# Low halves behind the residual, gains of the second attention folded into other steps, and a new order of head work, in a two-block transformer kernel

## What is computed

```python
def diff_mixer(h, cos, sin, w_in, w_out, q_norm, k_norm, lam_params, out_norm, lam_init):
    q, k, v = jnp.split(h @ w_in, [qk_w, 2 * qk_w], axis=-1)
    q = partial_rope(rms_norm(q.reshape(...), q_norm), cos5, sin5)   # 8 heads x 2 maps of 64
    k = partial_rope(rms_norm(k.reshape(...), k_norm), cos5, sin5)   # first 16 of 64 columns turned
    lam = exp(sum(lp[0] * lp[1])) - exp(sum(lp[2] * lp[3])) + lam_init
    p = masked_softmax(q k^T * scale, causal)
    a = p[:, :, 0] - lam * p[:, :, 1]
    o = rms_norm(a @ v, out_norm) * (1.0 - lam_init)
    return o @ w_out
```

## Time and profile before

| | us |
|---|---|
| median of 3 runs | 1537.43 |
| profiled execution, its own time | 1539.54 |
| its span | 1537.7 |
| PE busy | 1461.9 (95%) |
| DVE busy | 1060.2 (69%) |
| ACT busy | 757.7 (49%) |

### The profile page before, as it was taken

The page is one execution under the profiler, slowest core; times in us unless marked ns, Lnnn a source line. Parts: engine busy times, 40 slices in busy tenths (PEclk is TensorE's granted clock), DMA queues, the critical chain, the costliest instruction groups (busy, mean ns, idle before and its releaser), DMA issues.

```text
span 1537.7 us, 21173 instructions
## 1 busy us (share of the span) xinstructions
PE 1461.9 (95%) x8545; PEld 1185.5 (77%) x8545; DVE 1060.2 (69%) x1637; ACT 757.7 (49%) x1208; POOL 0.2 (0%) x4
## 2 busy tenths in 40 slices
PE   5998999999998899999989999989999998999997
PEld 3777778888786567787768888778888886788886
DVE  4586768886769866566576655688877897476555
ACT  3454554344544554334446554465546635465543
POOL 0000000000000000000000000000000000000000
PEclk9999999999999999999999999999999999999999
DMA  9875367876465758875855755568876523246551
GB/s 363 302 257 219 111 200 253 284 275 232 152 246 194 245 193 294 300 274 201 299 193 203 235 190 194 193 209 272 280 282 217 196 79 110 83 137 192 180 196 76
DMA packets 167842, 331.05 MB, mean 215 GB/s; under 512 B 8120, under 2 KB 109120, under 8 KB 167744
## 3 DMA queue, kind: packets, MB, share of 16 engines
q1 hardware_dynamic: 140928, 230.90, 44.6%
q10 hardware_dynamic: 26816, 98.79, 17.5%
HBM read 328.61 MB, written 1.05 MB: 214 GB/s over the span
## 4 chain that ended last, share of the span: by engine, by line
PE 80%; DVE 12%; DMA 3%; ACT 2%; issue 2%; SPq 0%; ACTq 0%; DVEq 0%
PE ps L2097 21%; PE ps L1991 13%; PE ps L1992 13%; PE ps L1993 13%; PE ps L2098 11%; PE ps L1928 2%; DVE wlo L1221 2%; DVE res L1321 1%; PE ps L2177 1%; DVE work L1319 1%; DMA work<-in_pool_scale_dram 1%; PE ps L2280 1%; DMA ring<-in_ada_w_dram 1%; DVE hT L1392 1%; DMA work<-in_ada_w_dram 1%
## 5 line engine op out<-in xcount | busy, mean ns | idle before, releaser
L1221 DVE TENSOR_TENSOR wlo<-wraw,whi 128x1024 fp32r<-128x1024 f32 (+1 forms) x410 | 481.4, 1216 | 139.7 <-ACT whi L685 138.8
L685 ACT ACTIVATE whi<-wraw 128x1024 fp32r<-128x1024 f32 (+1 forms) x410 | 409.4, 1047 | 330.1 <-PE ps L2098 198.9
L2097 PE MATMUL ps<-hT,whi 128*128 128x512 f32 x1472 | 524.5, 401 | 2.2 <-DVE hT L1392 2.2
L2098 PE MATMUL ps<-hT,wlo 128*128 128x256 f32 x1472 | 413.4, 281 | 0.0
L2097 PEld LDWEIGHTS ps<-hT,whi 128*128 128x128 f32 x1472 | 277.4, 188 | 78.8 <-issue 7.4
L2098 PEld LDWEIGHTS ps<-hT,wlo 128*128 128x128 f32 x1472 | 278.6, 189 | 0.0
L1991 PE MATMUL ps<-whi,act_hi 128*128 128x512 f32 x560 | 219.1, 391 | 0.0
L1992 PE MATMUL ps<-wlo,act_hi 128*128 128x512 f32 x560 | 218.0, 389 | 0.0
L1993 PE MATMUL ps<-whi,act_lo 128*128 128x512 f32 x560 | 217.9, 389 | 0.0
L1991 PE MATMUL ps<-whi,hT 128*128 128x512 f32 (+2 forms) x416 | 160.7, 386 | 6.3 <-DVE hT L1392 5.7
L1992 PE MATMUL ps<-wlo,hT 128*128 128x512 f32 (+2 forms) x416 | 158.3, 380 | 0.0
(11 more groups left out here) (237 smaller groups left out, 1293.2 us busy)
## 6 DMA issues: line engine op xcount, KB each, us to landing
wraw<-in_mlp_w_dram SPq DMA_DIRECT2D x96, 1024.0 KB, 5.4
ring<-in_ada_w_dram ACTq DMA_DIRECT2D x78, 1024.0 KB, 6.6
wraw<-in_ffn_w_gate_dram SPq DMA_DIRECT2D x22, 1024.0 KB, 5.4
wraw<-in_ffn_w_up_dram SPq DMA_DIRECT2D x22, 1024.0 KB, 6.5
wraw<-in_ffn_w_down_dram SPq DMA_DIRECT2D x22, 1024.0 KB, 4.9
wraw<-in_diff_w_in_dram SPq DMA_DIRECT2D x12, 1024.0 KB, 5.2
work<-in_ada_w_dram ACTq DMA_DIRECT2D x10, 1024.0 KB, 10.3
wraw<-in_sp_w_in_dram SPq DMA_DIRECT2D x8, 1024.0 KB, 8.5
```

The source lines that it names most:

```text
L685: nc.scalar.activation(whi[:, u % 2, part], raw_view(u)[:, part], ACT.Copy).then_inc(hi_ready, 1)
L1221: nc.vector.tensor_tensor(wlo[:, u % 2, part], raw_view(u)[:, part], whi[:, u % 2, part].bitcast(F32), ALU.subtract).then_inc(lo_ready, 1)
L2097: mm(ps[:, bank, :], whi[:, u % 2, c0:c0 + P], hT[:, :, k, :], start=(k == 0), stop=False, skip_group_check=True)
L2098: ins = mm(ps[:, bank, 0:S], wlo[:, u % 2, c0:c0 + P], hT_hi[:, k, :], start=False, stop=(k == KT - 1), skip_group_check=True)
```

## The change

It does the following.

- **Joins.** DVE's low part of the next segment's first unit is taken out of `row_segment` (`hold=2`) and `stream`. Its first half stands in `norm` between the residual and the inverse roots, its second half between the scaling and the modulation. For `out1`'s second unit the low halves stand in the attention's steps 8 and 10. ACT's copies keep their places. 32 of the 60 idle products go.
- **Second attention.** The gains of queries and keys are no longer multiplied over the rows: for the 16 turned columns they are folded into tables of cosines and sines (`trig1`), for the rest into the copies after the turn, as a column (`gain_qk`, loaded by four small DMAs on SyncE's queue). Lambda moves into `in1_0` and `in1_1`. PE turns queries 0, 1, 2 ahead of the gate and waits for half of the panel only.
- **Output of the second attention.** ACT takes a square root (its table is loaded in step 7), DVE the reciprocal and one round; DVE scales tile 0 in 4 instructions and ACT tile 1 in 8; the output gain, a column `gain_c`, goes into the two instructions that split.
- **First attention's head.** The gate goes ahead of group 3; the block sums are 8 instructions; `vector_out(3)` goes behind two parts of the query heads; the copies of groups 5 and 7 move; ACT loads the table of exponentials early.

```diff
@@ constants
+        HEAD_BANKS = (0, 1, 3, 2, 0, 1, 3, 6)
+        HEAD_ORDER = (0, 1, 2, 4, 5, 6, 3, 7)
-        IDLE_NORM = {1: 7, 2: 6, 4: 2, 10: 5}
-        IDLE_GATE = {1: 5, 2: 6, 4: 4, 9: 6}
-        IDLE_HEADS = {1: 5}
-        IDLE_ROWS = 4
+        IDLE_NORM = {1: 2}
+        IDLE_GATE = {1: 5, 4: 4, 9: 6}
+        IDLE_ROWS = 1
@@ ScalarE
+                    act.wait_ge(sem("a1_squares"), a.steps)
+                    n = TT * a.steps
+                    nc.scalar.activation(nwt[:, 32:32 + n], stat[:, 0:n], ACT.Sqrt, scale=1.0 / HD2, bias=eps_c[:, 0:1]).then_inc(sem("a1_rooted"), 1)
+                    act.wait_ge(sem("a1_inverse"), 1)
...
+            def scaled_rows(b):
+
+                for h in (2 * b, 2 * b + 1):
+                    o = r1[:, 1, h * P:(h + 1) * P]
+                    ins = nc.scalar.activation(o, o, ACT.Copy, scale=rstat[:, TT * h + 1:TT * h + 2])
+                ins.then_inc(sem("rows1_act"), 1)
...
             ring_fill(40)
+            act.wait_ge(sem("gain_columns"), 1)
+            for g in (0, 1, 2):
+                turned_head(g)
             gate()
-            turns(1)
-            attention(1)
-            out_turn(1)
+            for g in (5, 3):
+                turned_head(g)
+            attention(1, beside=lambda i: root_table() if i == 7 else None)
+            gained_out_turn()
@@ VectorE
-                    if i < s_["count"] - 1 or not hold_last:
+                    if i < s_["count"] - 2 or not hold_last:
                         split_unit(s_["base"] + i + 2)
...
-            def norm():
-                norm_rows()
+            def norm(first=None):
+
+                if first is not None:
+                    low_half(first, 0)
+                norm_roots()
+                norm_scaled()
+                if first is not None:
+                    low_half(first, 1)
                 norm_columns()
...
             nc.vector.memset(hidr[:, :], 0.0).then_inc(sem("hidr_zero"), 1)
-            vector_out(3)
             nc.vector.memset(cmp_s, NEG)
             heads0(1, (0, 1))
+            vector_out(3)
+            heads0(1, (2,))
             turns(0, 4, 6)
-            heads0(1, (2,))
-            turns(0, 6, 8)
             heads0(1, (3,))
...
+            late_unit = by_name["out1"]["base"] + 1
+            attention(1, beside=lambda i: low_half(late_unit, 0) if i == 8 else low_half(late_unit, 1) if i == 10 else None)
...
-            rsqrt(n)
-            for h in range(ATT[1].steps):
-                for t in range(TT):
-                    o = r1[:, t, h * P:(h + 1) * P]
...
+            link(nc.vector.reciprocal(y, nwt[:, 32:32 + n]))
+            link(nc.vector.tensor_tensor(z, y, y, ALU.mult))
+            link(nc.vector.tensor_tensor(z, z, x, ALU.mult))
...
+            for b in range(4):
+                o = r1[:, 0, 2 * b * P:(2 * b + 2) * P].rearrange("p (h d) -> p h d", h=2)
@@ TensorE
-            gate()
-            idle_products(IDLE_BANK, IDLE_HEADS[1])
+            pe.wait_ge(sem("query_heads1"), 1)
+            turned_heads1((0, 1, 2))
+            gate(tiles=1)
             pe.wait_ge(sem("heads1"), 1)
-            turns(1)
-            turned(1)
+            turned_heads1((4, 5, 6))
+            pe.wait_ge(dve_emptied, dve_count[8])
+            turned_heads1((3, 7))
```

More of the change, by code:

```diff
@@ new lines, in _ @@
+            row_segment("in1_0", heads=first_panel)
+            panel_rows(r1, 0, 1024)
+            held_split("in1_0")
+            row_segment("in1_1", heads=second_panel)
+            panel_rows(r1, 1024, 1024)
+            held_split("in1_1")
+            heads1(0, 3)
+            nc.vector.memset(mark[:, 1:2], 0.0).then_inc(sem("query_heads1"), 1)
+            row_segment("in1_2", heads=lambda i: heads1(1, i) if i < 3 else None)
+            heads1(1, 3)
+            nc.vector.memset(mark[:, 1:2], 0.0).then_inc(sem("heads1"), 1)
```

191 lines of the change are left out of this document (128 added, 63 removed).

## The result

| | before | changed |
|---|---|---|
| median of 7 runs, us | 1540.25 (1534.49 to 1546.16) | 1529.81 (1523.83 to 1534.12) |
| ratio, 95% interval | | 0.9935 (0.9916 to 0.9954) |
| span of the profiled execution | 1537.7 | 1527.3 |
| PE / DVE / ACT busy | 1461.9 / 1060.2 / 757.7 | 1451.4 / 1050.2 / 760.0 |

The change makes the kernel faster by 0.65%, some 10 us. The forecast was 18 us and 1519.4; the median lies 1.8 above the range's upper end (1528.0). The direction is right, the size is a little over half of what was forecast.

What follows compares the result with a forecast made beforehand. PE held 80% and DVE 12% of the last-ending path; only that 12% and PE's idle time could be won. Joins 9.7 plus heads 8.35 made 18 us, so a median of 1519.4, range 1511.5 to 1528.

Steps and rivals of the forecast that it cites:

- First attention's head: Compression before the first attention: the later `vector_out(3)` fits in PE's wait of 2.95; 0, bounds −2.0 and +1.5.
- Second attention: Head and output of the second attention: scores start earlier, 6.6 us, and a shorter root and shared scaling, 1.75.
- rival 3: Second attention: scores don't start early because ring loads come late; half of 6.6 left, 1523 to 1526; chance 15%.
- `out1`: Join of `out1`: residual in step with PE 2.0, plus gate idle time and clock; 3.2 us, bounds 1.6 and 3.7.
- The sentence about the DMA share of 0.99: Join of `out1`: DMAs are busy there, so the next vectors' load may set its own end; no size given.
- The other joins: Joins besides `out1`: low halves moved from in front of the residual, partly hidden by former waits; 6.5 us together.
- `out0`: Join of `out0`: DVE was early there, so the moved halves cost more than the slack; −1.0 us.
- `down0`: Join of `down0`: slack 2.5, less 0.5 for each half that shows; written as +1.0 us.
- `down1`: Join of `down1`: second half hidden by a turn wait of 1.81, pooling scale's DMA unmoved; +1.3 us, bounds 0 and 2.0.
- rival 2: At each join both low halves stay on the path, 2.36 removed and 2.36 added; about 1530; chance 9%.
- Rival 1: Clock falls at nine places that lose idle products, 3 us each, 27 in all; about 1546, slower; chance 4%.
- Rival 4: Clock recovers at two or three more joins where PE idles less, 1.7 to 3 us each; 1511 to 1515; chance 14%.

Runs made afterwards that it cites:

- e10: The kernel before with only `vector_out(3)` moved behind the first two parts of the query heads; from `in0` to `out0` 81.82 us, against 81.50.
- e1: The changed kernel with `vector_out(3)` back ahead of the query heads, nothing else; median 1523.39 us, ratio 0.9906 to the kernel before.
- e0: The changed kernel run once more with nothing edited, nine runs; median 1527.62 us.
- e4: On top of e1, the weight loads of `up1`'s vector issued in the first step of `out1` instead of the second; median 1523.71 us.
- e6: On top of e1, idle products ahead of turns and rows restored as in the kernel before; median 1.7 us below e1.
- e7: On top of e1, all idle products removed (28 more); median 1.9 us above e1.
- e8: The changed kernel with the edits of e1 and e4, and that of e5 at `pool0` alone; median 1518.37 us, ratio 0.9873.
- e5: On top of e1, the low half of the pooling segments' first unit back ahead of the residual at both pooling joins; median 3.4 us below e1.
- e3: The changed kernel with the joins' low halves put back ahead of the residual, heads and idle products as changed; 5.9 us below the kernel before.

## Why the prediction was wrong in size

- **First attention's head, forecast 0, measured −4.1.** This is the step that failed. I argued that `vector_out(3)` comes 1.8 later and fits in PE's later wait of 2.95, and three things in it were wrong. The row comes 2.9 later in the changed kernel and 3.3 in e10. I took the 1.6 of rows 12 for PE's idle time ahead of the compression; it is DVE's wait for PE, and PE's own was 0.59. And I took the rows of PE's work from the old order, where in the new one PE is done 1.8 earlier. So the idle time became 5.33 where I had named 3.4, and the compression fell to the 1.2 GHz level, which cost 2.5. My lower bound was −2.0, "compression runs slower", and the forecast gave it no weight. That e10, with the line late in the old order, lost 0.3 and so nearly bears out the 0 is luck: its scores came 1.2 later, and a missing stretch at the lower clock gave 0.9 back. e1: without the late line the head gains 1.5, my upper bound.
- **Second attention, forecast 8.35, measured 6.2.** Every step of the working held: the scores came 6.6 earlier, and the output's turn took 6.43 from the last vector to `out1` (529.82 to 536.25), before 8.31, so 1.9 for 1.75. What the stretch lacks against e1, 2.4, is rival 3 in part: waits for ring loads (1.00 and 1.30; before one of 1.63), and a fall of the clock behind one. In e1, with 0.96 and 0.37 and no fall, the stretch gains 8.6. I had put rival 3 at half of the head's gain, through later scores; it came later, inside.
- **`out1`, forecast 3.2, measured 1.8 (0.4 in e0).** The residual came into step as worked out (2.4 of the slack of 2.5), the clock came back, and the load I had named as a possible end was the end. e4 took it away: 3.3. Then the order is worth 1.6 where I had 2.0. The sentence about the DMA share of 0.99 deserved a number in the sum, not a mention.
- **The other joins, forecast 6.5, measured 7.6** (without `in1`'s 0.3 and what `up0` gained): the total is near, by luck. For `out0`, `down0`, `out1`, `down1` with `pool0` and `pool0` my sum had 5.1 for the order and 1.2 for the clock; at the full clock the order brought 3.2, and the clock 3.7. At `down0` my own terms, 2.5 − 0.5 − 0.5, give 1.5 and I wrote 1.0; measured 1.2. At `down1` I had 1.3: the join got 1.0 shorter at the full clock and `pool0` behind it 0.95 longer, for the second half stands ahead of what PE waits for. I had counted the turn waits as cover for the second half. They covered what they measured, but then no wait was left, so a part of both halves shows (rival 2's mechanism, which alone would have left nothing).
- **`out0`, forecast −1.0:** the join lost 0.8. `up0` behind it ran 1.2 shorter, which no step foresaw: its first eleven units ran at the faster of the two paces below.
- **Rival 1 (the clock falls where the idle products were) did not happen:** the mean granted clock is 0.988 over the sixteen runs of the changed kernel and 0.987 over the 28 of the kernel before beside e0. By the Trainium skill's page "TensorE: Matmul & The Clock Gate", section "Why this matters for your kernels", PE shouldn't be left idle for long between bursts. The trace agrees where the idle time was 5.33, three times of three; 3.93 had no fall in its one profile. Of the short idle times of 1.56 and 1.96, which went both ways, the page's row says nothing, so the row at `out1` was no support for it. Its core, that such products hold the clock, is borne out by e6 and e7; the price that I gave it, 3 us at each of nine places, is not.
- **Rival 4 (the clock recovers at the joins) came true in part:** 3.7 us at three joins. The losses above outweighed it.
- **Untouched segments, forecast 0, measured −1.8.** They carry the clock and the pace below. No term of mine had them, and they were as large as the terms I argued about.

## What to carry to other kernels

When a change moves work on two engines at once, take an engine's free time from the new order of both. A wait that hid a step before the change hides it no longer once the other engine is early too. Compare two kernels only at the same granted clock: at `out1` a comparison across the clock and a load's landing would have put the moved halves at 0.1, and they are worth 1.6. Before a stretch is credited with the whole of a shorter chain, ask what else lands there: at `out1` and in the attention it was a load, and issuing it one step earlier or keeping another off the queues brought what the reordering alone didn't. And compare segments, not totals, where single terms are of 1 to 2 us: start and clock move totals by more.

## What the runs showed of the hardware

**Two paces at full clock.** Long stretches of units ran at one of two speeds, with a granted clock of 1.00: a unit of `up3` took 5.653 us in seven profiles and 5.547 in six, constant over the units behind the first, so 1.6 us in 179. `up20` had the same two values. e1 had the faster one in `up3` and the slower in `up20`, e8 the faster in both. The pace can change inside a segment, and did so near a place where other matmuls stand between two units: in `up0` the changed kernel ran the first eleven units at 5.55 and the later ones at 5.65, e1 the first thirteen at 5.65 and the next ones at 5.55, and the kernel before all of them at 5.65. Both paces came with the same code (`up3` is the same in e4 and e5). What sets it stays open.

**The stretches at the lower clock** were 3.4 or 6.8 us long in these profiles, but for the one at the program's end. Their price depends on what stands in them: 1.6 in `down1`, where PE has work all through it, 1.7 before `pool0` (e7), 1.0 at `down0` (e3 against the kernel before), 0.6 at `out1` (the kernel before against e10), and 2.5 for the longer one in the compression. Idle time ahead of them isn't enough to tell: 1.56 (before against e3 and e10, at `out1`), 1.96 (`down1`, both ways) and 3.93 (e10, no fall) stand against 5.33 (a fall each time). The same kernel had most of them at the same places in two executions, and at two more joins in the second.
